# The order of matrix products that use one half of the TensorE array: delta-rule inverse, pairwise attention scores and weighted values

## The reference, cut to what matters

```python
s = einsum(q * 64**-0.5, k) + bias          # per head, 256 queries x 512 keys
p = softmax(s);  out = einsum(p, v)         # v: 512 keys x 64
```

```python
a = m + jnp.eye(C)                                        # C = 64, per chunk and head
u_c = lax.linalg.triangular_solve(a, vb, ...)
w_c = lax.linalg.triangular_solve(a, kb * exp(gc), ...)
```

## Time and profile before

| | |
|---|---|
| median of 3 runs | 3143.33 us |
| lowest, highest | 3133.09, 3146.02 us |
| the profiled execution: its span, first to last instruction | 3134.3 us |
| PE busy | 3017.0 us, 96% |
| PE weight loads busy | 2841.8 us, 91% |
| DVE busy | 2015.1 us, 64% |
| ACT busy | 1233.1 us, 39% |
| DMA queue 1 | 57.5% of the span of 16 engines |

### The profile page before, as it was taken

One profiled execution on the slowest core, in us unless ns is written; L12 is line 12 of the kernel. 1 busy time (PEld: TensorE's weight loads), 2 busy tenths in 40 slices (PEclk: granted clock), 3 DMA queues, 4 the chain that ended last, 5 costly groups with the idle time before them and its releaser, 6 DMA issues.

```text
span 3134.3 us, 55278 instructions
## 1 busy us (share of the span) xinstructions
PE 3017.0 (96%) x23638; PEld 2841.8 (91%) x23638; DVE 2015.1 (64%) x2887; ACT 1233.1 (39%) x1633; POOL 338.9 (11%) x331
## 2 busy tenths in 40 slices
PE   7999998999999998998999999999999999999999
PEld 4888987999999777998999999889999998997998
DVE  4686685777775786677646754666565576446754
ACT  2222223545443333434544412445454443134543
POOL 5000001101011121003110010011020102000301
PEclk9999999999999998998998999999999999999999
DMA  7354343799995665997655512346575663232664
GB/s 265 111 165 143 116 155 111 212 259 276 257 267 166 198 189 169 262 282 205 184 166 155 151 46 77 98 146 186 168 197 165 172 164 81 69 97 83 185 172 125
DMA packets 747377, 524.77 MB, mean 167 GB/s; under 512 B 19370, under 2 KB 711788, under 8 KB 747004
## 3 DMA queue, kind: packets, MB, share of 16 engines
q1 hardware_dynamic: 743004, 516.18, 57.5%
q0 software_dynamic: 4128, 5.06, 0.6%
HBM read 520.07 MB, written 2.94 MB: 167 GB/s over the span
## 4 chain that ended last, share of the span: by engine, by line
PE 78%; DVE 9%; ACT 6%; issue 5%; DMA 1%; SPq 0%; POOL 0%; DVEq 0%; ACTq 0%; POOLq 0%
PE bank L496 21%; PE bank L497 20%; PE bank L498 20%; ACT weights_hi L466 4%; PE bank L1439 2%; PE bank L618 2%; DVE weights_lo L476 1%; DVE conv_out L2273 1%; PE bank L2440 1%; PE bank L2452 1%; PE bank L2448 1%; PE bank L843 1%; PE bank L1444 1%; PE bank L1459 1%; PE bank L1513 1%
## 5 line engine op out<-in xcount | busy, mean ns | idle before, releaser
L476 DVE TENSOR_TENSOR weights_lo<-weights_raw,weights_hi 128x2048 fp32r<-128x2048 f32 (+3 forms) x414 | 854.2, 2064 | 370.0 <-ACT weights_hi L466 369.5
L466 ACT ACTIVATE weights_hi<-weights_raw 128x2048 fp32r<-128x2048 f32 (+3 forms) x414 | 709.4, 1714 | 686.8 <-PE bank L498 565.9
L496 PE MATMUL bank<-ffn_in_hi,weights_hi 128*128 128x256 f32 x1184 | 343.6, 290 | 14.5 <-DVE ffn_in_lo L1217 8.6
L497 PE MATMUL bank<-ffn_in_lo,weights_hi 128*128 128x256 f32 x1184 | 339.7, 287 | 0.0
L498 PE MATMUL bank<-ffn_in_hi,weights_lo 128*128 128x256 f32 x1184 | 339.4, 287 | 0.0
L496 PE MATMUL bank<-mac_in_hi,weights_hi 128*128 128x256 f32 x1024 | 289.6, 283 | 1.5 <-DVE mac_prod L2056 1.1
L498 PE MATMUL bank<-mac_in_hi,weights_lo 128*128 128x256 f32 x1024 | 289.0, 282 | 0.0
L497 PE MATMUL bank<-mac_in_lo,weights_hi 128*128 128x256 f32 x1024 | 289.0, 282 | 0.0
L496 PE MATMUL bank<-mix_in_hi,weights_hi 128*128 128x256 f32 x960 | 282.4, 294 | 6.2 <-DVE mix_in_lo L1957 3.7
L497 PE MATMUL bank<-mix_in_lo,weights_hi 128*128 128x256 f32 x960 | 275.0, 286 | 0.0
L498 PE MATMUL bank<-mix_in_hi,weights_lo 128*128 128x256 f32 x960 | 274.8, 286 | 0.0
(11 more groups left out here) (442 smaller groups left out, 7437.4 us busy)
## 6 DMA issues: line engine op xcount, KB each, us to landing
weights_raw<-in_ffn_w SPq DMA_DIRECT2D x132, 512.0 KB, 6.2
weights_raw<-in_w_in SPq DMA_DIRECT2D x120, 512.0 KB, 5.1
side_weights<-in_ada_w SPq DMA_DIRECT2D x86, 576.0 KB, 4.5
weights_raw<-in_ffn_wg SPq DMA_DIRECT2D x88, 512.0 KB, 4.0
weights_raw<-in_ffn_wu SPq DMA_DIRECT2D x88, 512.0 KB, 5.3
weights_raw<-in_ffn_wd SPq DMA_DIRECT2D x64, 704.0 KB, 4.6
weights_raw<-in_ffn_w SPq DMA_DIRECT2D x48, 704.0 KB, 7.0
side_weights<-in_ada_w SPq DMA_DIRECT2D x112, 256.0 KB, 3.3
```

The lines of the kernel that those rows point to most:

```text
L466: k.s.activation(k.w_hi[s % HIGHS][:, 0:n], k.raw[s % RING][:, 0:n], ACT.Copy).then_inc(*k.hi.up())
L476: k.v.tensor_tensor(k.w_lo[s % RING][:, 0:n], k.raw[s % RING][:, 0:n], k.w_hi[s % HIGHS][:, 0:n].bitcast(F32), ALU.subtract).then_inc(*k.l ...
L496: k.te.matmul(out, l[0], r[0], start=first, stop=False)
L497: k.te.matmul(out, l[0], r[1], start=False, stop=False)
```

## The change

In `pe_inverse`, the two loops of every group are swapped: the heads are the outer loop and the halves the inner one, so that products on the first and the second half of the array take turns. The corner steps are as before. In `pe_pairs`, the four score products are issued first, in the order 0, 2, 1, 3, which alternates the heads and so the halves, and then the four bias products in the order 0, 1, 2, 3; each bias product raises `scored` as before. In `weighted`, the loop over heads goes inside the loop over the parts of the sum, and both waits on the copies stand ahead of all of it. The number of products, their operands and their banks are as before.

```diff
     def keys(self, k, bank, e, tt):
         r = slice(e * DA_DH, (e + 1) * DA_DH)
         n = self.width(tt)
         k.te.matmul(bank[:, 0:n], k.pair_q[r, tt * P:(tt + 1) * P], k.pair_k[r, 0:n], start=True, stop=False)
+
+    def biased(self, k, bank, e, tt):
+        n = self.width(tt)
         if self.na:
...
-    def weighted(self, k, bank, e, n):
-        r = slice(e * DA_DH, (e + 1) * DA_DH)
+    def weighted(self, k, bank, n):
+        heads = [(e, slice(e * DA_DH, (e + 1) * DA_DH)) for e in range(2)]
         if self.na:
             for s in range(4):
-                m = k.te.matmul(bank[r, 0:T], k.pair_v_all[:, s, self.at(e, n)], k.pair_pt[:, e, s, :], start=s == 0, stop=s == 3)
+                for e, r in heads:
+                    m = k.te.matmul(bank[r, 0:T], k.pair_v_all[:, s, self.at(e, n)], k.pair_pt[:, e, s, :], start=s == 0,
+                                    stop=s == 3)
             return m
-        k.te.matmul(bank[r, 0:T], k.pair_v_all[:, 0, self.at(e, n)], k.pair_pt[:, e, 0:T], start=True, stop=False)
-        return k.te.matmul(bank[r, P:T], k.pair_v_all[:, 1, self.at(e, n)], k.pair_pt[:, e, T:TRI], start=False, stop=True)
+        for e, r in heads:
+            k.te.matmul(bank[r, 0:T], k.pair_v_all[:, 0, self.at(e, n)], k.pair_pt[:, e, 0:T], start=True, stop=False)
+        for e, r in heads:
+            m = k.te.matmul(bank[r, P:T], k.pair_v_all[:, 1, self.at(e, n)], k.pair_pt[:, e, T:TRI], start=False, stop=True)
+        return m
...
+        for i in (0, 2, 1, 3):
+            m.keys(k, k.AB[i], i // 2, i % 2)
         for i in range(4):
-            m.keys(k, k.AB[i], i // 2, i % 2).then_inc(*m.scored.up())
+            m.biased(k, k.AB[i], i // 2, i % 2).then_inc(*m.scored.up())
...
-        for e in range(2):
-            te.wait_ge(*m.even_kept.at(2 * n + e + 1))
-            te.wait_ge(*m.odd_kept.at(2 * n + e + 1))
-            x = m.weighted(k, bank, e, n)
-        x.then_inc(*m.valued.up())
+        te.wait_ge(*m.even_kept.at(2 * n + 2))
+        te.wait_ge(*m.odd_kept.at(2 * n + 2))
+        m.weighted(k, bank, n).then_inc(*m.valued.up())
...
-            for r in ROWS:
-                for i in range(DN_H):
+            for i in range(DN_H):
+                for r in ROWS:
                     m = te.matmul(AB[2 * tt + 1][r, BLK[i]], XTc[r, tt, i, :], Y[tt][r, i, :], start=True, stop=True)
             m.then_inc(*k.inv_right.up())
...
```

## The result

| | before | after |
|---|---|---|
| median of 4 runs each | 3138.44 us (3133.09 to 3146.02) | 3041.09 us (3034.23 to 3045.56) |
| ratio, 95% interval | | 0.9684 (0.9657 to 0.9711) |
| span of the profiled execution | 3134.3 us | 3032.9 us |
| mean granted clock of it | 0.965 | 0.971 |

The change takes 3.2% off the time: 101.4 us between the two profiled spans, 97.4 us between the medians. An execution's time is 1.3 us above its span in these runs (3034.23 beside 3032.9), so most of the 9.0 us that I had put between span and median was not something around the span; the profiled execution of before was quicker than most.

A forecast was written before the change was run, and what follows sets the result against it. PE, busy 3017.0 of 3134.3 us, was taken as the bound, with DVE near in neighbourhood pairs. Inverse 38, dilated pairs 21.5 and neighbourhood pairs 18.5 sum to 78 off: span 3056, plus 9.0 gives 3065, range 3045 to 3102.

The forecast's parts named there:

- The halves overlap: Inverse: about 3 of 16 passes of a half already overlap at each change of half, counted as 55 and 107 slots.
- The inverse: Levels fall from 15.77 to 11.94 us with halves in turn; 38 us saved in all.
- `da`: Dilated pairs: keys of both heads overlap, saving 1.80 us a pair over 12 pairs, taken as 21.5 us.
- Weighted values at nothing: Dilated pairs: weighted values already overlap and hide behind the wait for `pair_q`, so they save 0.
- PE in `na`: Neighbourhood pairs: PE alone would save 2.87 us on scores plus 0.9 on weighted values, 3.8 a pair.
- All rivals: Keys not overlapping 0.10; issue floor 0.11; slower strict turns 0.05; waits absorbing gains 0.05; same-bank halves taking turns 0.03.
- the pricing: Sampled stretches of the touched stages run almost wholly at 2.4 GHz, so all terms were priced at that clock.
- `na`'s size: Neighbourhood pairs, bound by DVE: 2.2 us for five, 3.2 for three, less 2 for side weights, 18.5 us.
- The base: Whole kernel: the runs' median of 3143.3 us lies 9.0 above the profiled span, a distance kept in the forecast.
- The range: Whole kernel: 3045 us, with neighbourhood pairs bound by PE at 30 instead of 18.5, to 3102.

The follow-up runs named there:

- a third order: The whole change with inverse halves taking turns after four products instead of each one: 3070.93 us, ratio 0.9762.
- the whole change: All edits of the change together against the kernel before, run again on another occasion: 3044.78 us, ratio 0.9689.
- An edit of two loop headers: Kernel before with halves in turns only in the turning step of the inverse: 3132.09 us, ratio 0.9975.
- the inverse alone: Kernel before with halves in turns in the inverse's turning step and every level, pairs as before: 3099.64 us, ratio 0.9863.

## Why the prediction was right in most steps and 24 us off

**The halves overlap**, by the count of slots: right, and shown for a third order. **The inverse**: 38 forecast, 39.9 at full clock alone. **`da`**: every 9.7 us forecast and measured, where it was 11.53. Weighted values at nothing: right, their 0.5 us stand as before. **PE in `na`**: 2.88 a pair for the scores, 2.87 forecast. All rivals fell. The Trainium skill (TensorEngine Tiling (Array Packing), Restrictions and Gotchas), by which different row tiles can't access one PSUM bank at a time, differs from the runs here: groups of one bank take 0.93 for 32 passes, 0.029 each, level after level. The 62 ns a MATMUL that the Trainium skill gives for decoding in microcode (TensorE: Matmul & The Clock Gate, Wait — 56ns, not 53.3ns?) did not bind here, by the same 0.029.

**The step that failed** is the pricing: "The granted clock is 1.00, 0.97 and 1.00 in these stretches, so almost everything runs at 2.4 GHz and is priced there." I had read single stretches of 20 to 95 us, and two of the three show no fall. The mean of the whole profile was 0.965 before, which is some 220 us at half clock, and part of that stood in the stages of the change: between 42 and 53 us in each of the three profiles of before, 15 and 26 in two of the whole change. So the sum lacked a term: time at half clock that leaves with the change. Over all runs it is 35 us at half clock (234 before, 200 after), worth 17.4 us if half of each is lost, and 14 by the 0.41 measured at the end. I had named a lower clock as what would break the pricing; it went the other way. What drives the fall in the first level of the inverse is shown as far as said above; why the pairs lose theirs stays open. In `na` one case can be seen: of the pairs with side sums on PE, three had the clock down for 3.4 us before, behind the one-column products of L618, and took 23.3 to 23.4 us; after, the first still falls (21.7 us), and the other two take 18.1.

**`na`'s size**: non-finishing pairs went from 20.6 to 20.97 down to 17.8 to 18.1, 2.8 to 2.9 a pair, where the sum had 2.2, less 2 us in all for DMAs. A pair with side sums and no fall in either kernel went from 21.85 to 18.12, 3.7, which is PE's own saving. Three inputs were off. The sum gave 3.2 to three pairs and 2.2 to five, though five of the eight have side sums; the other way round its own figures give 22.6 and not 20.6. The maxima are 0.60 apart, not 0.69: I took a record's length for its distance, against what I did for PE, which made the 5.3 too long by 0.2. And the side weights held DVE up less than before, not more. Two groups of DVE's work over the last six `na` pairs (shapes, count, busy us, mean ns), before and after, with the idle time ahead of them last:

```profile
L587 DVE SCALAR_TENSOR_TENSOR side_sums<-side_weights,silu_c,side_sums 128x1152 f32<-128x1152 f32 x9 | 12.7, 1416 | 3.6 <-DMA side_weights<-in_ada_w 3.3
L587 DVE SCALAR_TENSOR_TENSOR side_sums_odd<-side_weights_third,silu_c,side_sums_odd 128x1152 f32<-128x1152 f32 x4 | 7.1, 1764 | 1.6 <-DMA side_weights_third<-in_ada_w 1.4
```

```profile
L587 DVE SCALAR_TENSOR_TENSOR side_sums<-side_weights,silu_c,side_sums 128x1152 f32<-128x1152 f32 x9 | 13.7, 1518 | 1.3 <-DMA side_weights<-in_ada_w 1.1
L587 DVE SCALAR_TENSOR_TENSOR side_sums_odd<-side_weights_third,silu_c,side_sums_odd 128x1152 f32<-128x1152 f32 x4 | 5.6, 1410 | 0.2
```

The pairs are shorter and yet DVE waits less for these transfers; the core moved 241 GB/s over this stage where it moved 204. What freed the DMAs I did not test. At full clock the whole gained 80.3 against 78, so all sizes together were 2.3 off; by the price at the end of this document (0.41 us for each us at half clock), 5.

**The base**: the median of three runs, 3143.3, was 2 to 4 us above the medians of 11 to 13 runs (3139.3, 3141.3, 3140.5). So 3065 - 3041.1 = 24 us are 17 of clock, 2 of sizes, and about 5 of base and scatter. The last number is what is left, not measured by itself.

**The range** was also not what its terms give: `na` at 30 instead of 18.5 leads to 3053.5 and not 3045, and the upper bound of the inverse, levels of 11.17 instead of 15.77, is 46 us and not 41. The measured 3041 lies below all of these, and the term of the clock alone is larger than the 4 us by which it missed.

## What to carry to other kernels

In these runs half-array products of both halves overlapped when the other half's next product stood within three (inverse) or four (scores) passes in program order, one bank or not; so put them in turns, split no product in a way that lengthens the run of one half, and keep full-array products out from between them. Before pricing an edit of PE's work, sum the time at half clock over the stages that it touches, not over one sample stretch, and give its going or coming a term of its own. And look at what paces the stage next, pair by pair: the last 0.9 us a pair of PE's saving in `na` was worth about a quarter in all, nearly the whole where PE has side sums and almost nothing where DVE was the bound already.

## What was unexpected of the hardware

With two short steps of the inverse run on one half at a time, behind a wait of PE, the granted clock fell in 7 of 8 inverses for 6.8 to 10.2 us; with one or both of them in turns, in 0 of 20, although the shorter products leave PE idle longer in between. An edit of two loop headers, forecast at 1 us at full clock, took 8 us of 3140; but the inverse alone, which has the same edit and more, shows no such gain of the clock over its six runs, so the 8 us should not be counted on elsewhere. Also, runs of one and the same kernel differ by their clock: over the 35 runs of before the mean clock went from 0.955 to 0.968, and a run with 1 us more at half clock was 0.41 us longer (0.36 in the ten of the whole change). "At full clock" is worked out with 0.5, which is then too much: the whole change has 35 us less at half clock, and by 0.41 that is 14 us and not 17.4, with 83 instead of 80.3 at full clock.
